# A linear-attention recurrence's decays and bonus sums moved into the stages beside them, and its triangular inverses laid out by the parity of the head

## The chip, the cores and the metric

The kernel runs on one core of a Trainium2 chip. Its time is the device time of one execution in microseconds; a kernel is timed several times and the median stands for it. Lower is better. A profiled execution is one such run with the hardware profiler on.

## The reference, cut to what matters

The program is a block of one layer (a mix of sliding-window attention and an RWKV-7 recurrence, then a gated feed-forward) followed by two more layers. All is float32, 512 tokens, width 1024. The change touches the recurrence of layer one alone:

```python
def rwkv7_time_mix(p, ...):                       # p: 512 tokens x 1792 columns of the projection
    r, k, v, zw, za, zg = jnp.split(p, RWKV_SPLITS, axis=-1)
    w_log = -jax.nn.softplus(-(w0 + jnp.tanh(zw) @ w_decay_up)) - 0.5
    decay = jnp.exp(-jnp.exp(w_log))
    a = jax.nn.sigmoid(a0 + za @ w_iclr_up)
    g = jax.nn.sigmoid(zg) @ w_gate_up
    kk = normalised (k * k_k) per head of 64
    k = k * (1.0 + (a - 1.0) * k_a)
    def step(state, inp):                         # 8 heads, state 64 x 64 each
        sa = einsum('bhvk,bhk->bhv', state, -kk_t)
        state = state * w_t + sa * (kk_t * a_t) + v_t * k_t
        return state, einsum('bhvk,bhk->bhv', state, r_t)
    o = normalised per head, times ln_x_g plus ln_x_b
    bonus = jnp.sum(rh * kh * r_k, axis=-1, keepdims=True) * vh
    return (o + bonus) * g
```

The kernel does the recurrence in 8 chunks of 64 tokens. Inside a chunk the state's own feedback is a unit lower triangular system of 64 x 64 per head, whose inverse it builds by doubling; r, k, kk and aa (= kk times a) are first scaled by running products of the decays, so that inside a chunk plain matrix products remain.

## The kernel before, in words

Heads come in pairs: partition half q (0 or 1) and column block hh (0 to 3) of a [128, 4, 512] tensor hold head 2*hh+q. A token tile t (0 to 3) has 128 tokens, two chunks c of 64.

`first_stage` (line 1658) is the projection. TensorE (PE) goes through 20 tiles m of 128 output columns, each 8 k-steps of three passes (high and low halves of weights and input: lines 325 to 327). Beside each tile, in an order written out by hand through numbers such as RANK, MIX, KSQUARE and KSUM, run the units of the windowed attention (starting, turning, summing), the low-rank products (L1827), the running sums of the log decays (L2034, `scanned`), a's scaling of k (L2036, L2038), and kk's normalisation: squares on ScalarE (ACT, L1959), a head-wise sum on PE with the constant `pair` (L1836, at tiles 16 to 19), a lower bound on VectorE (DVE, L2042), Ln and Exp on ACT (`root`), and two products on DVE (`unit_key`, L1994 and L1995), the last of them after the loop. PE waits for `bounded(i)` before the head-wise sum i, for i of 1 and more. ACT makes the high half of the weights two tiles ahead (L308), GpSimd (POOL) the low half from it (L312), SyncE (SP) loads them.

`rwkv` (line 1263) is three stages with a barrier between each. The first (c1, lines 1269 to 1308) makes the decays' exponentials ep and em on ACT, the last column of each chunk pc, the sigmoid of the gate, on DVE r*r_k*k (L1300), kk times ep and aa times em (L1304, L1305), on PE the head-wise bonus sums (L1295) and on DVE their product with v (L1308).

The second (c2, from line 1314) runs a list `order` of (kind, t, level). Step n uses the PSUM bank pair n mod 4, and PE waits until step n-4 is taken out. A step's 64 x 64 products are issued in the order CROSSED; DVE or ACT (kinds in BY_ACT) take the result out. nt is aa with kk (row half q, column half c of PE, bank q), masked; p0 turns nt by 16 products with the identity, and DVE masks it and adds the identity matrix in a second instruction (L1514, L1515); POOL makes the other orientation Tt from nt in two instructions a tile (L1374, L1376), after its k times em and r times ep (L1370, L1371). Eight `turn` steps bring v, k, aa and kk to token rows (L1418) with ACT copies of 1024 columns. Then come five doubling levels: p (nt with T, masked by DVE, L1517), tt (added by DVE, L1519), t (T is Tt turned by 16 products with the identity, copied by ACT, L1555; not at the last level). p, tt, t, p0, y and u use row half c and column half c only, so halves (0,0) and (1,1) in turn. After them ak (like nt, for k), y, w and u lead into the loop over the 8 chunks (lines 1459 to 1499), in which PE also carries a share of the output projection (`half_tile`, L1448 to L1450). The third stage (from line 1567) normalises and gates.

CROSSED before walks the four halves in two runs, so 8 products go to (0,0) and (1,1) in turn, then 8 to (0,1) and (1,0):

```python
CROSSED = [(x, y, hh) for two in (((0, 0), (1, 1)), ((0, 1), (1, 0))) for hh in range(4) for x, y in two]
```

Of the kernel before, what the change touches and what calls it, by code (L numbers as in the profile page):

```python
# [7 lines left out]
ALU = mybir.AluOpType  # L8
# [121 lines left out]
def _program(nc, a, out, whole):  # L130
# [1132 lines left out]
    def rwkv(r, k, v, zg, aa, kk, decay, oT, attended, f):  # L1263

        with ExitStack() as ctx:
            cs, ep, em, vt = (sb(ctx, n, [P, 4, S]) for n in ("cs", "ep", "em", "vt"))
            masks = sb(ctx, "masks", [P, 10, C])
            pc = sb(ctx, "pc", [P, 4, NCH])
            with ExitStack() as c1:
                s_in, expd, pr, bsum = (sig(n) for n in ("s_in", "expd", "pr", "bsum"))  # L1270
                block = c1.enter_context(stage())

                def ends(m):
                    return ep[:, m, :].rearrange("p (c t) -> p c t", t=C)

                @block.sync
                def _(sp):
                    cst_dma(sp, masks[:, :, :].rearrange("p l n -> p (l n)"), "packed", s_in)
                    sp.wait_ge(s_in.h, 16)

                @block.scalar
                def _(act):
                    for m in range(4):
                        act.activation(ep[:, m, :], decay[:, m, :], ACT.Exp, scale=-EHALF).then_inc(expd.h, 1)
                        act.activation(em[:, m, :], decay[:, m, :], ACT.Exp, scale=EHALF).then_inc(expd.h, 1)
                    for m in range(4):
                        act.wait_ge(expd.h, 2 * m + 1)
                        act.activation(pc[:, m, :], ends(m)[:, :, C - 1], ACT.Copy)
                    act.activation(zg[:, :], zg[:, :], ACT.Sigmoid)

                @block.tensor
                def _(pe):
                    for m in range(4):
                        pe.wait_ge(pr.h, m + 1)
                        pe.matmul(bank[4 + m][:, :], pair, cs[:, m, :], start=True, stop=True).then_inc(bsum.h, 1)  # L1295

                @block.vector
                def _(dve):
                    for m in range(4):
                        pr.by(dve.scalar_tensor_tensor(cs[:, m, :], r[:, m, :], col("r_k", m), k[:, m, :], ALU.mult, ALU.mult))  # L1300
                    for m in range(4):
                        kc = kk[:, m, :].rearrange("p (c t) -> p c t", t=C)
                        dve.wait_ge(expd.h, 2 * m + 2)
                        dve.tensor_tensor(kc[:, :, 1:C], kc[:, :, 1:C], ends(m)[:, :, 0:C - 1], ALU.mult)  # L1304
                        dve.tensor_tensor(aa[:, m, :], aa[:, m, :], em[:, m, :], ALU.mult)  # L1305
                    for m in range(4):
                        dve.wait_ge(bsum.h, m + 1)
                        dve.tensor_tensor(cs[:, m, :], bank[4 + m][:, :], v[:, m, :], ALU.mult)  # L1308
# [6 lines left out]
            with ExitStack() as c2:  # L1315
# [6 lines left out]
                made, took, copied, seeded, uppered, lowered = (  # L1322
                    sig(n) for n in ("made", "took", "copied", "seeded", "uppered", "lowered"))
# [4 lines left out]
                order += [("turn", x, 0) for x in range(8)]  # L1328
# [14 lines left out]
                CROSSED = [(x, y, hh) for two in (((0, 0), (1, 1)), ((0, 1), (1, 0))) for hh in range(4) for x, y in two]  # L1343
# [5 lines left out]
                def at(q, hh):  # L1349
                    return slice(q * HALF + hh * C, q * HALF + hh * C + C)  # L1350

# [17 lines left out]
                def pool_part(pool):  # L1369
                    pool.tensor_tensor(k[:, :, :], k[:, :, :], em[:, :, :], ALU.mult).then_inc(decayed.h, 1)  # L1370
                    pool.tensor_tensor(r[:, :, :], r[:, :, :], ep[:, :, :], ALU.mult).then_inc(decayed.h, 1)  # L1371
                    for t in range(NT):
                        wait_taken(pool, where["nt", t, 0])
                        pool.tensor_tensor(four(Tt[:, t, :]), four(nt[:, t, :]), mask(TURNED), ALU.mult).then_inc(seeded.h, 1)  # L1374
                        pool.wait_ge(seeded.h, 2 * t + 1)
                        pool.tensor_tensor(four(Tt[:, t, :]), four(Tt[:, t, :]), mask(EYE), ALU.add).then_inc(seeded.h, 1)  # L1376
# [8 lines left out]
                def _(sp):  # L1385
                    for c in range(NCH):
# [3 lines left out]
                def _(pe):  # L1390
                    for n, (kind, t, l) in enumerate(order):
# [3 lines left out]
                        if kind == "p0":  # L1395
                            wait_taken(pe, where["nt", t, 0])
# [1094 lines left out]
```

## Time and profile before

| | us |
|---|---|
| median of 3 runs | 2296.46 (2294.19 to 2296.58) |
| the profiled execution | 2295.25 |
| its span, first to last instruction | 2293.5 |
| PE busy in it | 2167.7 (95%) |
| PE weight loads | 1747.6 (76%) |
| DVE busy | 1220.4 (53%) |
| POOL busy | 997.1 (43%) |
| ACT busy | 859.3 (37%) |

Times in the profile are microseconds from the span's start, unless marked ns. A record is one instruction on one engine. A product of fp32 operands leaves two matmul records (PE) and two weight-load records (PEld); a transpose leaves one of each. A record's duration holds its latency, so for products in a stream the distance between starts is what counts.

### The profile page before, as it was taken

To read this page: it belongs to the slowest core of one execution; us is meant where nothing else is said; L and a number is where in the kernel's file an instruction comes from. 1 tells how busy PE (TensorE), PEld (TensorE's weight loads), DVE (VectorE), ACT (ScalarE), POOL (GpSimd) and SP (SyncE) were. 2 spreads that over 40 slices of the span, in tenths; PEclk is the share of its full clock that TensorE was granted. 3 is DMA by queue.
4 is the path that set the end of the run, shared out by engine and by line. 5 is a ranking of instruction groups with operands and counts; after the bars stand their busy time and mean duration, and the time that the engine had idled before them with its cause. 6 is when DMAs were issued, how large, how long until landed. Compare 5 with 4: busy or idle time off the path is not lost. (4 is left out here: it accounts for less than half of the span.)

```text
span 2293.5 us, 35211 instructions
## 1 busy us (share of the span) xinstructions
PE 2167.7 (95%) x13161; PEld 1747.6 (76%) x13161; DVE 1220.4 (53%) x1928; ACT 859.3 (37%) x1345; POOL 997.1 (43%) x524
## 2 busy tenths in 40 slices
PE   6997998799999999899889999999999889999998
PEld 4676985688888888777667888888677668888887
DVE  3456525677505772331774577721397664777601
ACT  3455124433313332332364433332323744333322
POOL 4224011244544444365653444444365734444442
PEclk9998998799999999899999999999999989999999
DMA  4220012133332333333102333333332003333232
GB/s 126 65 65 25 4 32 58 57 101 101 109 92 83 99 93 101 87 83 81 48 1 74 92 91 100 96 94 94 86 86 80 1 20 92 96 101 96 87 101 87
DMA packets 347085, 177.10 MB, mean 77 GB/s; under 512 B 20835, under 2 KB 344158, under 8 KB 346974
## 3 DMA queue, kind: packets, MB, share of 16 engines
q1 hardware_dynamic: 346476, 175.47, 26.7%
q8 instruction: 75, 1.23, 0.2%
q14 instruction: 36, 0.29, 0.0%
q10 hardware_dynamic: 210, 0.08, 0.0%
q0 software_dynamic: 288, 0.03, 0.0%
HBM read 173.44 MB, written 2.11 MB: 77 GB/s over the span
## 5 line engine op out<-in xcount | busy, mean ns | idle before, releaser
L312 POOL TENSOR_TENSOR wlo<-raw,whi 128x1024 fp32r<-128x1024 f32 (+3 forms) x347 | 792.3, 2285 | 1085.4 <-ACT whi L871 605.8
L325 PE MATMUL banks<-xhi,whi 128*128 128x512 f32 x1688 | 669.3, 396 | 6.7 <-DVE cb L1034 3.9
L326 PE MATMUL banks<-xlo,whi 128*128 128x512 f32 x1688 | 659.0, 390 | 0.0
L327 PE MATMUL banks<-xhi,wlo 128*128 128x512 f32 x1688 | 659.0, 390 | 0.0
L325 PEld LDWEIGHTS banks<-xhi,whi 128*128 128x128 f32 x1688 | 318.2, 189 | 82.4 <-issue 13.7
L326 PEld LDWEIGHTS banks<-xlo,whi 128*128 128x128 f32 x1688 | 318.3, 189 | 68.5 <-issue 3.9
L327 PEld LDWEIGHTS banks<-xhi,wlo 128*128 128x128 f32 x1688 | 318.0, 188 | 67.3
L961 ACT ACTIVATE cb<-banks,conv 128x512 f32<-128x512 f32 x152 | 118.0, 779 | 440.8 <-DVE banks L1023 440.8
L871 ACT ACTIVATE whi<-raw 128x1024 fp32r<-128x1024 f32 (+2 forms) x208 | 205.0, 989 | 186.2 <-DMA raw<-in_ffn_w_out_dram 80.6
L325 PE MATMUL banks<-ghi,whi 128*128 128x512 f32 x608 | 236.5, 389 | 0.0
L327 PE MATMUL banks<-ghi,wlo 128*128 128x512 f32 x608 | 236.5, 389 | 0.0
L326 PE MATMUL banks<-glo,whi 128*128 128x512 f32 x608 | 236.5, 389 | 0.0
L1023 DVE TENSOR_TENSOR banks<-banks,rs 128x512 f32<-128x512 f32 x152 | 106.0, 699 | 171.6 <-PE banks L327 154.2
L1042 DVE CAST ghi<-gv 128x512 f32 (+1 forms) x76 | 167.1, 2199 | 10.4 <-DVE gv L1040 2.6
L308 ACT ACTIVATE whi<-raw 128x1024 fp32r<-128x1024 f32 (+3 forms) x139 | 134.6, 970 | 61.8 <-DMA raw<-in_ffn_w_out_dram 22.2
L326 PEld LDWEIGHTS banks<-glo,whi 128*128 128x128 f32 x608 | 114.2, 188 | 23.8
L325 PEld LDWEIGHTS banks<-ghi,whi 128*128 128x128 f32 x608 | 114.1, 188 | 23.6
L327 PEld LDWEIGHTS banks<-ghi,wlo 128*128 128x128 f32 x608 | 114.2, 188 | 23.6
L1034 DVE SCALAR_TENSOR_TENSOR cb<-banks,conv,cb 128x510 f32<-128x510 f32 x152 | 113.8, 749 | 18.3 <-DVE cb L1032 0.3
L1032 DVE SCALAR_TENSOR_TENSOR cb<-banks,conv,cb 128x511 f32<-128x511 f32 x152 | 112.7, 741 | 7.2 <-ACT cb L961 7.2
L1065 DVE TENSOR_TENSOR xT<-banks,xT 128x512 f32 x16 | 11.1, 692 | 191.5 <-PE banks L327 191.5
L1144 POOL TENSOR_SCALAR ex<-ex,mx 128x128 f32<-128x128 f32 (+3 forms) x64 | 70.9, 1122 | 37.9 <-DVE mx L1222 37.9
(450 smaller groups left out, 2619.4 us busy)
## 6 DMA issues: line engine op xcount, KB each, us to landing
raw<-in_ffn_w_in_dram SPq DMA_DIRECT2D x88, 512.0 KB, 3.9
raw<-in_w_ffn_up_dram SPq DMA_DIRECT2D x64, 512.0 KB, 4.1
raw<-in_w_ffn_down_dram SPq DMA_DIRECT2D x32, 512.0 KB, 3.8
raw<-in_ev_w_in_dram SPq DMA_DIRECT2D x25, 512.0 KB, 3.9
raw<-in_ffn_w_out_dram SPq DMA_DIRECT2D x32, 384.0 KB, 3.4
raw<-in_ffn_w_out_dram SPq DMA_DIRECT2D x32, 320.0 KB, 3.3
raw<-in_od_w_in_dram SPq DMA_DIRECT2D x20, 512.0 KB, 3.9
raw<-in_w_in_dram SPq DMA_DIRECT2D x16, 512.0 KB, 3.8
```

The costliest lines, as they stand in the source:

```text
L308: w_hi.by(act.activation(whi[s % CUT][:, 0:n, :], raw[s % RAW][:, 0:n, :], ACT.Copy))
L312: return pool.tensor_tensor(wlo[c][:, 0:n, :], raw[b][:, 0:n, :], whi[c][:, 0:n, :].bitcast(F32), ALU.subtract)
L325: pe.matmul(acc, whi[b][:, k, :], hi(k), start=first and k == 0, stop=False)
L326: pe.matmul(acc, whi[b][:, k, :], lo(k), start=False, stop=False)
L327: mm = pe.matmul(acc, wlo[b][:, k, :], hi(k), start=False, stop=last and k == n - 1)
L871: act.activation(whi[s % CUT][:, 0:n, :], raw[s % RAW][:, 0:n, :], ACT.Copy).then_inc(w_hi.h, 1)
L961: act.activation(cb[j][:, :], bank[j][:, :], ACT.Identity, scale=conv[:, 2, bass.ds(c, 1)], bias=conv[:, 3, bass.ds(c, 1)])\
L1023: dve.tensor_tensor(bank[j % 4][:, :], bank[j % 4][:, :], rs, ALU.mult).then_inc(scaled.h, 1)
L1032: chain(dve.scalar_tensor_tensor(cb[j][:, 1:S], bank[j][:, 0:S - 1], conv[:, 1, bass.ds(c, 1)], cb[j][:, 1:S], ALU.mult, ALU.add))
L1034: dve.scalar_tensor_tensor(cb[j][:, 2:S], bank[j][:, 0:S - 2], conv[:, 0, bass.ds(c, 1)], cb[j][:, 2:S], ALU.mult, ALU.add).then_inc(conve ...
L1042: dve.tensor_copy(ghi[:, i * 2 + q, :], gv[q][:, :]).then_inc(upper.h, 1)
L1144: ins = pool.tensor_scalar(e[:, g, 0:w], e[:, g, 0:w], mx[u % 4][:, 2, g:g + 1], None, ALU.mult)
```

## The change

In `first_stage`: the head-wise sums for kk go from tiles 16 to 19 to tiles 14 to 17 (KSUM 14), so the last `root` and `unit_key` run at tile 18, and the table load for Ln and Exp goes from tile 17 to tile 14. New beside the tiles: r*r_k*k into cs on DVE at tiles 13, 14, 16 and 18; at tiles 15 and 16 ep and em of column blocks 0 and 1 and their part of pc on ACT; one tile later kk times ep and aa times em on DVE; at POOL's turns 18 and 19 k times em and r times ep of a block; the gate's sigmoid as a Tanh on ACT and a scaling on DVE. cs shares its memory with qT.

In `rwkv`: stage c1 is gone. c2 begins with ep and em of blocks 2 and 3 on ACT, kk times ep and aa times em on DVE; PE waits for both blocks (keyed 2), and POOL scales k and r of both blocks. The bonus sums are two steps `bonus` of `order`, evacuated by DVE. p0 is the product of kk and aa in swapped roles instead of a turn of nt. nt, T and pm have the parity of the head as partition half where the products allow it; Tt comes from T, and T from Tt, by four 128 x 128 transposes and one ACT copy of 512 columns; POOL's eight instructions for Tt are gone. nt, p0 and p use all four halves of PE in turn (MIRRORED, PAIRED), and CROSSED, which tt, y, w, u, ak and two places of the chunk loop use (L1475, and L1495 with L1498), is one walk of all four:

```diff
-                order += [("turn", x, 0) for x in range(8)]
+                order += [("turn", 0, 0), ("turn", 1, 0), ("bonus", 0, 0), ("bonus", 1, 0), ("turn", 6, 0), ("turn", 7, 0)]
+                order += [("t", t, 0) for t in range(NT)]
+                order += [("turn", x, 0) for x in (4, 5, 2, 3)]
...
-                CROSSED = [(x, y, hh) for two in (((0, 0), (1, 1)), ((0, 1), (1, 0))) for hh in range(4) for x, y in two]
+                CROSSED = [(x, y, hh) for hh in range(4) for x, y in ((0, 0), (1, 1), (0, 1), (1, 0))]
+                MIRRORED = [(q, hh, c) for c in range(2) for i in range(2) for q, hh in ((0, 2 * i), (1, 2 * i + 1), (0, 2 * i + 1), (1, 2 * i))]
+                PAIRED = [(x % 2, c, x // 2 // 2, 2 * (x // 2 % 2) + x % 2) for i in range(4)
+                          for x, c in ((2 * i, 0), (2 * i + 1, 1), (2 * i, 1), (2 * i + 1, 0))]
...
+                    pool.wait_ge(expd.h, 4)
+                    pool.tensor_tensor(k[:, 2:4, :], k[:, 2:4, :], em[:, 2:4, :], ALU.mult).then_inc(decayed.h, 1)
+                    pool.tensor_tensor(r[:, 2:4, :], r[:, 2:4, :], ep[:, 2:4, :], ALU.mult).then_inc(decayed.h, 1)
...
+                pe.wait_ge(keyed.h, 2)
...
+                        elif kind in ("nt", "p0"):
+                            x, y = (aa, kk) if kind == "nt" else (kk, aa)
+                            for q, hh, c in MIRRORED:
+                                mm = pe.matmul(two[q][part(hh % 2), hh // 2 * P + c * C:hh // 2 * P + (c + 1) * C],
+                                               x[part(q), hh, toks(t, c)], y[part(q), hh, toks(t, c)], start=True, stop=True)
...
+                        elif kind == "t":
+                            for x in range(4):
+                                mm = pe.transpose(two[0][:, x * P:(x + 1) * P], (Tt if l else T)[:, t, x * P:(x + 1) * P], ident)
+                        elif kind == "p":
+                            for x, c, q, hh in PAIRED:
+                                mm = pe.matmul(two[x][part(c), (2 * q + hh // 2) * C:(2 * q + hh // 2 + 1) * C],
+                                               nt[part(x), t, side(q, hh, c)], T[part(x), t, side(q, hh, c)], start=True, stop=True)
...
+                    for i in (2, 3):
+                        dve.wait_ge(expd.h, 2 * i - 2)
+                        later = chunks(kk[:, i, :])[:, :, 1:C]
+                        dve.tensor_tensor(later, later, chunks(ep[:, i, :])[:, :, 0:C - 1], ALU.mult)
+                        dve.tensor_tensor(aa[:, i, :], aa[:, i, :], em[:, i, :], ALU.mult).then_inc(keyed.h, 1)
...
+                        if kind == "bonus":
+                            ins = dve.tensor_tensor(cs[:, 2 * t:2 * t + 2, :], banks[:, 2 * (n % 4):2 * (n % 4) + 2, :], v[:, 2 * t:2 * t + 2, :], ALU.mult)
...
+                            if t == 6:
+                                wait_taken(act, where["bonus", 1, 0])
...
-            RANK, MIX, KSQUARE, KSUM = 6, 8, 13, 16
+            RANK, MIX, KSQUARE, KSUM = 6, 8, 13, 14
+            BONUS, EXPS = (13, 14, 16, 18), 15
...
-                    if m == UNITS + 1:
+                    if m == RANK + 8:
                         act.preload_act_table_set("natural_log_exp_and_others")
```

## Rows read from the trace of the kernel before

**Rows 1.** Windows: stretch, its length, busy us (records) by engine, PE clock, DMA.
```profile
206.90:213.80 6.90, 5.78 (x164) 5.81 (x166) 3.86 (x7) 2.19 (x4) 5.51 (x2) 0.51 0.02 5
213.80:217.00 3.20, 2.87 (x100) 2.73 (x94) 3.05 (x2) 0.00 (x0) 3.20 (x1) 1.00 0.00 0
281.10:296.80 15.70, 13.68 (x519) 12.99 (x515) 3.29 (x6) 7.40 (x13) 0.00 (x0) 1.00 0.02 4
```

**Rows 2.** Timeline, inverses' stage: start, length, engine, line, tiles, count [idle before].
```profile
208.02 4.26 PE L1422 MATMUL banks<-kk,aa 64*64 64x64 f32 x122 [3.34 <-PEq L150]
...
212.80 4.52 POOL L1371 TENSOR_TENSOR r<-r,ep 128x2048 f32<-128x2048 f32 x1
...
214.64 3.23 DVE L1515 TENSOR_TENSOR f<-f,masks 128x512 f32<-128x512 f32 x1
...
225.02 1.93 ACT L1551 ACTIVATE em<-banks 128x1024 f32<-128x1024 f32 x2
225.65 1.91 PE L1418 MATMUL banks<-cst,kk 128*128 128x128 f32 x16
...
227.49 3.95 PE L1432 MATMUL banks<-f,oT 64*64 64x64 f32 x128
...
228.68 0.69 DVE L1517 TENSOR_TENSOR pm<-banks,masks 128x512 f32<-128x512 f32 x1 [5.77 <-PE banks L1432]
...
236.15 0.60 ACT L1555 ACTIVATE f<-banks 128x512 f32<-128x512 f32 x1 [7.36 <-PE banks L1430]
```

**Rows 3.** Timeline of PE, from ak into the chunk loop.
```profile
282.79 1.22 PE L1422 MATMUL banks<-kk,k 64*64 64x64 f32 x56
...
286.07 2.49 PE L1436 MATMUL banks<-vt,pm 64*64 64x64 f32 x78 [0.55 <-issue]
...
296.87 0.59 PE L1462 MATMUL banks<-z,kk 64*64 64x64 f32 x13 [0.95 <-ACT v L1555]
...
303.97 0.93 PE L1475 MATMUL banks<-r,k 64*64 64x64 f32 x29
```

**Rows 4.** Windows of PE alone: stretch, length, busy us (records), PE clock, DMA.
```profile
266.90:270.85 3.95, 3.85 (x126) 1.00 0.01 4
...
289.85:293.25 3.40, 3.08 (x127) 1.00 0.02 5
...
309.12:310.86 1.74, 1.74 (x68) 1.00 0.00 0
```

**Rows 5.** DMA view of 266.90 to 293.25: GB/s in 40 slices, and the only queue.
```profile
GB/s 0 0 25 0 0 0 0 25 0 0 0 0 0 25 0 0 0 0 0 0 25 0 0 0 0 25 0 0 0 0 25 0 0 0 0 0 25 0 0 0
...
q8 instruction: 7, 0.11, 1.8%
```

**Rows 6.** Timeline around tile 15 of the projection.
```profile
157.29 2.68 POOL L312 TENSOR_TENSOR wlo<-raw,whi 128x1024 fp32r<-128x1024 f32 x1 [3.67 <-ACT whi L308]
157.75 2.50 DVE L2036 TENSOR_SCALAR mixin<-aa,pcol 128x512 f32<-128x512 f32 x1
...
160.01 0.70 PE L1845 MATMUL banks<-kd,qT 64*128 64x256 f32 x4
```

**Rows 7.** Timeline, end of the projection and stage c1.
```profile
180.23 1.28 ACT L1961 ACT_TABLE_LOAD   x1
...
191.23 1.02 PE L1836 MATMUL banks<-sq,cst 128*128 128x512 f32 x2
...
192.95 0.75 DVE L2019 SCALAR_TENSOR_TENSOR v<-banks,pcol,v 128x511 f32<-128x511 f32 x1 [0.76 <-ACT v L1914]
...
196.55 0.69 DVE L1995 SCALAR_TENSOR_TENSOR aa<-aa,kk 128x512 f32<-128x512 f32 x1
...
197.77 0.63 ACT L1284 ACTIVATE ep<-oT 128x512 f32<-128x512 f32 x1 [2.15 <-PEq L150]
197.80 2.74 DVE L1300 SCALAR_TENSOR_TENSOR cs<-r,pcol,k 128x512 f32<-128x512 f32 x4 [0.56 <-PEq L150]
198.31 0.61 ACT L1285 ACTIVATE em<-oT 128x512 f32<-128x512 f32 x1
...
198.61 6.07 PE L1295 MATMUL banks<-cs,cst 128*128 128x512 f32 x8 [5.77 <-DVE cs L1300]
```

More of the change, by code:

```diff
@@ L1261, in _, with rwkv @@
                             exped.by(ins)
-    def rwkv(r, k, v, zg, aa, kk, decay, oT, attended, f):
+    def rwkv(r, k, v, zg, aa, kk, decay, cs, pc, oT, attended, f):
         with ExitStack() as ctx:
-            cs, ep, em, vt = (sb(ctx, n, [P, 4, S]) for n in ("cs", "ep", "em", "vt"))
+            ep, em, vt = (sb(ctx, n, [P, 4, S]) for n in ("ep", "em", "vt"))
             masks = sb(ctx, "masks", [P, 10, C])
[L1268 to L1308, printed above, removed]
@@ L1310, in rwkv, with chunks @@
+            def chunks(x):
+                return x.rearrange("p (c t) -> p c t", t=C)
             kt, bt, at_ = ep, em, v
@@ L1401, in _ @@
                             if l == 1:
-                                pe.wait_ge(seeded.h, 2 * t + 2)
+                                wait_taken(pe, where["t", t, 0])
                         elif kind == "t":
-                            wait_taken(pe, where["tt", t, l])
+                            wait_taken(pe, where["tt", t, l] if l else where["p0", t, 0])
                         elif kind == "y":
@@ L1410, in _ @@
                         two = bank[2 * (n % 4)], bank[2 * (n % 4) + 1]
-                        if kind == "turn":
+                        if kind == "bonus":
+                            for j in range(2):
+                                mm = pe.matmul(two[j], pair, cs[:, 2 * t + j, :], start=True, stop=True)
+                        elif kind == "turn":
                             src = (v, k, aa, kk)[t // 2]
@@ L1539, in _ @@
                 def _(act):
+                    for i in (2, 3):
+                        act.activation(ep[:, i, :], decay[:, i, :], ACT.Exp, scale=-EHALF).then_inc(expd.h, 1)
+                        act.activation(em[:, i, :], decay[:, i, :], ACT.Exp, scale=EHALF).then_inc(expd.h, 1)
+                    act.wait_ge(expd.h, 3)
+                    act.activation(pc[:, 2:4, :], ep[:, 2:4, :].rearrange("p i (c t) -> p i c t", t=C)[:, :, :, C - 1], ACT.Copy).then_inc(expd.h, 1)
                     for kk_ in range(4):
@@ L1553, in _ @@
                             ins = act.activation(wt[:, t, :, :, :], both(pr), ACT.Copy)
+                        elif kind == "t":
+                            ins = act.activation((T if l else Tt)[:, t, :], bank[2 * pr][:, :], ACT.Copy)
                         else:
-                            ins = act.activation(four({"t": T, "y": nt, "u": u0}[kind][:, t, :]), both(pr), ACT.Copy)
+                            ins = act.activation(four({"y": nt, "u": u0}[kind][:, t, :]), both(pr), ACT.Copy)
                         ins.then_inc(copied.h, 1)
@@ L1722, in first_stage @@
             AT_K = [ORDER1.index(("p", 4 + i)) for i in range(4)]
-            RANK, MIX, KSQUARE, KSUM = 6, 8, 13, 16
+            RANK, MIX, KSQUARE, KSUM = 6, 8, 13, 14
+            BONUS, EXPS = (13, 14, 16, 18), 15
+            AT_R = [ORDER1.index(("p", i)) for i in range(4)]
             def low_rank(m):
@@ L1940, in _ @@
                         act.activation(zt[0:HD, :], zt[0:HD, :], ACT.Tanh).then_inc(tanhed.h, 1)
+                    if m == AT_Z + 2:
+                        act.wait_ge(moved.h, AT_Z + 2)
+                        act.activation(zg[:, :], zg[:, :], ACT.Tanh, scale=0.5).then_inc(zgated.h, 1)
                     if m - 1 in AT_K:
```

83 lines of the change are left out of this document (52 added, 31 removed).

## The prediction

> **What bounds the kernel now.** The page's first part comes first: PE is busy for 95% of the span, so only PE's time counts. Where the edits lie that average is false. Read in order of time, PE ends its last projection tile at 191.2, does only the bonus products from 198.6 and begins the inverses at 208.0 [rows 2, 7]: 17 us with little in them. From 208.0 its clock is 1.2 GHz until 213.8, then 2.4 GHz [rows 1].
>
> In the doubling levels PE seems full: 128 records in 3.95 us, last latency 0.22 included, so (3.95 - 0.22)/127 = 29.4 ns a record and 0.94 us a step of 32 records (16 products) [rows 2]. Those steps use two halves of PE. The ak step uses all four, in two runs, and goes at (1.22 - 0.22)/55 = 18.2 ns [rows 3], so runs on different halves overlap. L1475, same order, averages 25.4 ns [rows 3].
>
> A second limit stands behind the halves. PE stops at 266.9 and six times after it, marked "issue", as at 286.07 [rows 3]. Between stops lie 126 or 127 matmul records, with their weight loads 256 instructions; the seven pieces end at 293.25, (293.25 - 266.90)/7 = 3.76 us each [rows 4]. In the same stretch the instruction queue brings seven blocks, evenly spaced [rows 5]. I read this as instruction supply: a block of 256 per 3.76 us, whatever PE could do. Even ak, whose 128 records need 2.3 us, is held to it.
>
> **The tail of the projection.** Four head-wise sums of kk move from tiles 16 to 19 to tiles 14 to 17. Each costs PE 0.9 (two records of 0.43) [rows 7]; four now stand ahead of the last tile's end instead of three, +0.9. PE must wait at tile 15 for `bounded`. DVE's tile 14 ends at 160.3 + 0.7 now, because L2036 is blocked behind POOL's weight split [rows 6]. In the change the table load (1.28, rows 7) stands ahead of the weights' high half, so POOL's split moves from 157.3 to some 159.3 and ends at 161.7; it blocks the new bonus product (0.69, a fourth of 2.74 in rows 7) instead, done at 162.3, and `bounded` at 163.0. PE would be ready at 160.0 + 0.9 = 160.9 [rows 6]: a stall of 2.1. Bounds: 0 if the bonus product gets ahead of POOL, 3 if another product of POOL falls in. The other new DVE work (two bonus products, 2 x 2 decays of 0.69) makes DVE one to two us late at tiles 17 and 18, which the distance between tiles hides, (191.2 - 160.0)/4 = 7.8 us [rows 6, 7]; POOL's four new products end before it is next needed. So the last tile ends at 191.2 + 0.9 + 2.1 = 194.2. After it no unit key is left, only scaling, tap and mix: 193.70 - 191.23 = 2.5. The stage ends at 196.7 instead of 197.24.
>
> **The c1 stage goes, and a wait comes.** ACT's first exponential now starts at 196.7 + 0.5 = 197.2. As in c1 the four take 0.54, 0.54, 0.52 and 0.6 [rows 7], so ep and em of block 2 are there after 1.15, of block 3 after 2.2. DVE does kk and aa of block 2 from 1.2 to 2.5. At 2.3 POOL is released by the same em. That DVE instructions with two operands in SBUF stand still for a whole POOL instruction is seen at 214.64: 3.23 us for 0.69 of work, until POOL's product of r ended at 217.3 [rows 2]. POOL's products have half of that size, 2.3. So POOL's k from 2.5 to 4.8, kk of block 3 to 5.4, POOL's r to 7.7, aa of block 3 to 8.35, and all of PE stands behind that wait. PE begins at 197.2 + 8.35 = 205.5 instead of 208.0: **gain 2.5**. Bounds: if DVE keeps its place, PE begins 4.7 earlier.
>
> **From nt to the first level** (now 227.5 - 208.0 = 19.5). nt and p0 run cold, 0.9 a step over four halves, against 4.04/121 x 32 = 1.07 now [rows 2]. The eight are done after some 7 us, but DVE takes p0 with two instructions a tile, 1.45, from 5.0 to 10.8. bonus 1 waits for the last: two fp32 products of 512 columns, 1.7, DVE's take-out 1.3 and 0.5 latency, 14.4. Only then may ACT overwrite v: six turns at 0.93 (two take 1.93, rows 2, less overlap) and four t copies of 0.55 make 7.8, to 22.2. That is when tile 3's p may start, 1.4 after a level's normal start, so level one starts at 20.9: **loss 1.4**. Bounds: loss 3, gain 1. POOL's eight instructions go off-path; their work is now in t.
>
> **Levels and ak to u** (227.5 to 296.9 = 69.4 now). Without the supply limit: p takes 0.47 a step (four halves, twice 29.4 ns' rate), 1.9 for four; tt, which keeps two halves, 3.75; t is four transposes at (1.91 - 0.27)/15 = 0.109, 0.44 a step, 1.75 [rows 2]. DVE takes a step in 0.69 and ACT in 0.60 [rows 2], inside the ring of four. A level is 7.4 instead of 11.2. With the limit: records are 128 + 128 + 16 = 272 a level, four times, 256 for the last, 512 for ak, y, w and u: 1856 = 14.5 blocks, against 2304 = 18.0 now (18 x 3.76 = 67.7, close to the 69.4 seen). One and a half blocks are in store after the slow turns, so 0.9 + 13 x 3.76 + 1.9 = 51.7, with the drain before the chunk loop (0.95 and a copy, rows 3) 1.3, and 1 for waits inside: 54.1. **Gain 15.3**: nearly all of it because t issues fewer instructions, not because p is faster. Bounds: 20.6 (no supply limit: four levels of 7.4, the last 1.9 + 3.75, ak and w at 0.6 a step by DVE's and ACT's pace and y and u at 0.94, 12.3, and the drain: 48.8) and 8.1 (first rival but one).
>
> The Trainium skill (Runtime: NRT & Kernel Launch, Instruction fetch mechanics) says that blocks of 256 instructions are fetched while the current one executes, and that this is hidden. The block's size agrees with the 256 counted between stops; "hidden" does not agree with stops at each of them. By the page the sum would be the upper bound, 20.6.
>
> **Chunk loop.** PE is the bound there. L1475's 32 records take 0.8 at its 25.4 ns [rows 3]; at ak's best rates or a little under them 0.5: 8 x 0.3 = 2.4. L1495 and L1498 take 1.74 for 64 records [rows 4]; now halves change every four products, overlap where they change: 1.2, four times 0.5. **Gain 4.5**, bounds -1.5 and 6.
>
> **Sum.** 2.5 - 1.4 + 15.3 + 4.5 = 20.9. From the profiled execution's 2295.25 (span 2293.5) that is 2274.4; the median is 1.2 above that execution, so **2275.5**. What follows after the third stage is unchanged; the clock's fall there can shift by 1 to 2 us.
>
> **Rivals.**
> - *The lock at the start of c2 doesn't bite.* DVE's four instructions stand back to back, so POOL may have to wait for them. Against: L2036 was blocked by a POOL instruction that came while DVE was at work [rows 6]. Gain 4.7 more: 2271.
> - *Supply is no limit*: the stops come from something else, or blocks are in store. For: no stops before 266.9. Gain 5.3 more: 2270.
> - *The new order overlaps nothing*: overlap comes from whole runs meeting, and alternation by single products is served strictly in order, 0.94 a step. p, nt, p0 gain nothing, ak and L1475 slow to 29.4 ns. Levels 4 x (3.75 + 3.75 + 1.75) + 7.5 = 44.5, ak to u 16.8: gain 8.1 instead of 15.3; chunks -1.5 instead of 4.5. Sum 7.7: 2289. For it: nothing in the trace alternates four halves by single products.
> - *Slower: neighbours in one row half exclude each other.* In the new order the load for (0,1) comes while (0,0) streams. If it must wait, each row half does load and stream in series: a 128-column transpose takes 109 ns [rows 2], so half of that, 55, for a record's stream, and some 27 for its load; over two row halves 41 ns a record, 1.31 a step. Twenty p steps make levels 52.2, ak to u 19.2: 71.4, loss 2; L1475, L1495 and L1498 lose 8 x 0.5 + 4 x 0.9 = 7.6; nt and p0, cold, lose 5. With 2.5 - 1.4: 13.5 slower, 2310. It decides from 33 ns a record on. Against: ak's 18.2 ns includes changes from (0,0) to (0,1) without such a price. The Trainium skill (TensorE: Matmul & The Clock Gate, Part 3) states this rule, that a weight load overlaps a running product only where the row group differs; by it ak would have been slower than p, and the rows say the reverse.
>
> **How the numbers follow.** The forecast holds with 0.51, its own range 2271 to 2281; lock rival 0.15, supply rival 0.12, no-overlap rival 0.13, row rival 0.04; 0.05 for a mix of stalls that ends between 2281 and 2292. Range for 8 in 10, from both fast rivals together to the no-overlap one: 2265 to 2289. A measurement tells 0.2% (4.6 us) from no change: faster 0.94, same 0.02, slower 0.04.
>
> **What would show it.** No stage between projection and inverses; PE's wait at tile 15 (2.1); PE's wait ended by DVE's aa at 8 us after ACT's exponential, with a DVE instruction of over 2 us; ak and p pieces near 15 to 18 ns a record; levels of some 8 us with "issue" stops every 128 matmul records from the first level on, and 54 us from first p to the chunk loop; 0.5 for L1475. Wrong would be p at 29 ns or above, levels of 7.4 without stops, or a time above 2289 or below 2265.

## The result, and the profile after

The changed kernel takes 2275.82 us (median of five runs, 2275.18 to 2276.84); the kernel before, run beside it, 2294.19 (2287.83 to 2296.58). The ratio is 0.9926 with a 95% interval of 0.9914 to 0.9939: 17 us faster, 14 to 20. The forecast of 2275.5 is met, but not every term of it, and part of the agreement is luck, as the table shows. It goes by the starts of the same instructions in both traces: VectorE's scaling of tile 12, ScalarE's first exponential behind the projection, the first product of nt, of level one, of the chunk loop, and of the third stage.

| stretch, us | before | after | difference | forecast |
|---|---|---|---|---|
| up to tile 12 | 136.4 | 139.3 | +2.9 | 0 |
| tile 12 to the exponential | 61.4 | 63.6 | +2.2 | -0.6 |
| exponential to nt | 10.2 | 3.7 | -6.5 | -1.9 |
| nt to level one | 19.5 | 21.3 | +1.8 | +1.4 |
| level one to the chunk loop | 69.4 | 60.5 | -8.9 | -15.3 |
| chunk loop to the third stage | 57.0 | 51.8 | -5.2 | -4.5 |
| third stage to the end | 1939.6 | 1934.9 | -4.7 | 0 |

The five stretches that the change can reach, all but the first and the last row, give 16.6 us instead of 20.9. The first and last row hold unchanged code. Over the fourteen profiled kernels of this case tile 12 is scaled at 135.5 to 139.3 and the last stretch takes 1929.4 to 1939.6, at mean granted clocks over the span of 0.971 to 0.978; so one profiled execution tells nothing of a few us there, and the net 1.8 that these two rows add is not the change's.

The page's busy times after; PE is busy for 2140.0 of 2275.1 us:

```profile
PE 2140.0 (94%) x12729; PEld 1721.0 (76%) x12729; DVE 1224.0 (54%) x1927; ACT 857.7 (38%) x1347; POOL 987.8 (43%) x520
```

Tile 15 in the changed kernel, answering to [rows 6] (timelines of DVE, POOL and PE):

```profile
162.51 2.75 DVE L2063 SCALAR_TENSOR_TENSOR cs<-r,pcol,k 128x512 f32<-128x512 f32 x1
165.18 0.68 DVE L2067 TENSOR_SCALAR roots<-banks 128x512 f32<-128x512 f32 x1
...
162.22 2.49 POOL L312 TENSOR_TENSOR wlo<-raw,whi 128x1024 fp32r<-128x1024 f32 x1 [5.68 <-ACT whi L308]
...
166.01 1.10 PE L1845 MATMUL banks<-sq,cst 128*128 128x512 f32 x2 [2.16 <-DVE roots L2067]
```

This is the stall of the forecast, of the forecast size (2.16 for 2.1): the bonus product lasts 2.75 us, until just after the end of POOL's weight split, for the 0.74 that it takes at 196.83 below; the bound (L2067) stands behind it, PE behind that.

The end of the projection and the start of the inverses' stage, answering to [rows 7]:

```profile
196.83 0.74 DVE L2063 SCALAR_TENSOR_TENSOR cs<-r,pcol,k 128x512 f32<-128x512 f32 x1
198.00 0.69 DVE L2012 SCALAR_TENSOR_TENSOR kk<-kk,mixin 128x512 f32<-128x512 f32 x1 [0.42 <-ACT mixin L1917]
198.73 1.65 DVE L2013 SCALAR_TENSOR_TENSOR aa<-aa,kk 128x512 f32<-128x512 f32 x1
200.41 0.70 DVE L2018 TENSOR_TENSOR banks<-banks,rs 128x512 f32<-128x512 f32 x1
201.86 0.75 DVE L2037 SCALAR_TENSOR_TENSOR v<-banks,pcol,v 128x511 f32<-128x511 f32 x1 [0.75 <-ACT v L1923]
204.09 0.68 DVE L1487 TENSOR_TENSOR kk<-kk,ep 128x504 f32<-128x504 f32 x1 [1.48 <-ACT em L1529]
204.69 0.69 DVE L1488 TENSOR_TENSOR aa<-aa,em 128x512 f32<-128x512 f32 x1
205.29 0.68 DVE L1487 TENSOR_TENSOR kk<-kk,ep 128x504 f32<-128x504 f32 x1
205.88 0.68 DVE L1488 TENSOR_TENSOR aa<-aa,em 128x512 f32<-128x512 f32 x1
...
198.56 1.26 POOL L312 TENSOR_TENSOR wlo<-raw,whi 128x512 fp32r<-128x512 f32 x1 [5.88 <-ACT whi L308]
206.81 2.38 POOL L1346 TENSOR_TENSOR k<-k,em 128x1024 f32<-128x1024 f32 x1 [6.99 <-issue]
...
204.48 0.61 ACT L1529 ACTIVATE em<-oT 128x512 f32<-128x512 f32 x1
...
197.21 0.39 PE L327 MATMUL banks<-xhi,wlo 128*128 128x512 f32 x1
...
206.62 3.69 PE L1396 MATMUL banks<-kk,aa 64*64 64x64 f32 x128 [8.44 <-DVE aa L1488]
```

Two things differ from the forecast. VectorE scales the last tile (L2018) at 200.41, though PE's last product of it, from 197.21 on, is done at 197.6: the last unit key stands before it, its second product (198.73, 1.65 us) once more held by a split. And VectorE's four decay products (204.09 to 206.57) are not blocked: POOL's product of k, released when the last exponential ends at 205.09, begins only at 206.81.

The levels, answering to [rows 2] and [rows 3] (timeline of PE):

```profile
227.90 2.19 PE L1407 MATMUL banks<-f,oT 64*64 64x64 f32 x128
229.91 1.92 PE L1413 MATMUL banks<-f,pm 64*64 64x64 f32 x60
232.35 2.21 PE L1413 MATMUL banks<-f,pm 64*64 64x64 f32 x68 [0.52 <-issue]
234.49 1.97 PE L1404 MATMUL banks<-cst,f 128*128 128x128 f32 x16
236.39 2.10 PE L1407 MATMUL banks<-f,oT 64*64 64x64 f32 x128
...
266.49 0.62 PE L1407 MATMUL banks<-f,oT 64*64 64x64 f32 x26 [1.35 <-issue]
...
270.54 1.03 PE L1413 MATMUL banks<-f,pm 64*64 64x64 f32 x28 [0.57 <-issue]
...
274.27 0.63 PE L1400 MATMUL banks<-kk,k 64*64 64x64 f32 x27 [1.18 <-issue]
...
278.33 1.09 PE L1415 MATMUL banks<-vt,pm 64*64 64x64 f32 x30 [0.63 <-issue]
...
282.34 0.63 PE L1419 MATMUL banks<-f,v 64*64 64x64 f32 x28 [1.46 <-issue]
...
286.16 1.27 PE L1417 MATMUL banks<-oT,f 64*64 64x64 f32 x33 [0.41 <-issue]
...
288.39 0.59 PE L1441 MATMUL banks<-z,kk 64*64 64x64 f32 x13 [0.95 <-ACT v L1553]
```

p (L1407) takes 2.19 for 128 records, (2.19 - 0.22)/127 = 15.5 ns each, about half of [rows 2]; t (L1404) 1.97 with its latency. But level one to level two is 8.49, and from 266.49 to 286.16 the restarts after stops are 3.93 us apart (3.73 to 4.06). One sign of the forecast came only in part: up to 266.49 PE stops once in two blocks (restarts at 232.35, 240.37, 248.66, 257.17 and 266.49, so 4.27 us a block), and at each block only from there on.

### The profile page after: what moved, and what is told of

The parts are those of the page before. It is cut to its first block and busy times, and to the rows that moved or that the text cites. A ratio compares the mean times of both kernels' runs of the same rounds, so it can differ in the third digit from the quotient of the medians.

```text
span 2275.1 us, 34323 instructions
## 1 busy us (share of the span) xinstructions
PE 2140.0 (94%) x12729; PEld 1721.0 (76%) x12729; DVE 1224.0 (54%) x1927; ACT 857.7 (38%) x1347; POOL 987.8 (43%) x520
## 5 line engine op out<-in xcount | busy, mean ns | idle before, releaser
L327 PEld LDWEIGHTS banks<-xhi,wlo 128*128 128x128 f32 x1688 | 318.1, 188 | 67.2
```

The costliest lines, as they stand in the source:

```text
L327: mm = pe.matmul(acc, wlo[b][:, k, :], hi(k), start=False, stop=last and k == n - 1)
```

## The experiments

Each kernel is the changed one with the edit shown; the times in the third column stand beside runs of the kernel before on the same chip.

| kernel | median us | ratio to before | tile 12 to exponential | to nt | to level one | to ak | to chunk loop | to third stage |
|---|---|---|---|---|---|---|---|---|
| changed kernel | 2275.82 | 0.9926 [0.9914, 0.9939] | 63.6 | 3.7 | 21.3 | 43.5 | 17.0 | 51.8 |
| bonus after bound | 2271.36 | 0.9911 [0.9889, 0.9933] | 61.7 | 3.7 | 21.3 | 43.7 | 15.7 | 51.8 |
| key after scaling | 2272.08 | 0.9917 [0.9899, 0.9935] | 62.7 | 3.7 | 21.3 | 41.3 | 15.6 | 51.8 |
| turns, bonus first | 2270.30 | 0.9904 [0.9885, 0.9923] | 63.7 | 8.3 | 14.8 | 41.7 | 16.5 | 51.9 |
| old order of halves | 2280.23 | 0.9947 [0.9930, 0.9964] | 63.6 | 3.7 | 21.3 | 42.2 | 17.0 | 57.0 |
| t twice | 2278.18 | 0.9938 [0.9921, 0.9956] | 63.6 | 3.7 | 20.1 | 46.6 | 16.7 | 51.9 |
| p twice | 2291.82 | 0.9997 [0.9987, 1.0007] | 63.6 | 3.7 | 21.3 | 60.9 | 16.8 | 51.8 |
| gap before block 3 | 2270.82 | 0.9900 [0.9882, 0.9918] | 65.0 | 4.3 | 20.9 | 42.9 | 15.6 | 51.8 |
| inverses and order alone | 2278.67 | 0.9938 [0.9920, 0.9956] | 61.4 | 10.3 | 21.5 | 42.4 | 17.0 | 51.8 |
| block 3 behind POOL | 2273.82 | 0.9920 [0.9902, 0.9939] | 63.6 | 9.6 | 19.7 | 42.1 | 15.7 | 51.8 |
| even spread | 2274.22 | 0.9923 [0.9909, 0.9936] | 63.6 | 3.7 | 13.2 | 51.0 | 16.2 | 51.9 |
| spread, bonus, key | 2267.32 | 0.9895 [0.9880, 0.9910] | 60.6 | 3.7 | 13.2 | 50.9 | 15.7 | 51.8 |
| spread to the stops | 2268.11 | 0.9885 [0.9869, 0.9901] | 60.6 | 3.7 | 12.1 | 51.0 | 17.5 | 51.8 |

How finely this can be read: the changed kernel and four of these (bonus after bound, key after scaling, gap, block 3) have the same PE instructions from nt to the chunk loop, and that stretch took 81.8, 80.6, 78.2, 79.4 and 77.4 us. So where instructions are fetched, one profile is good to 2 us to either side; the projection's columns and the chunk loop's repeat within 0.1, the gap kernel's 65.0 apart. The intervals of the ratios are 5 to 10 us wide. Even they claim too much: the gap kernel, which only adds a wait to the changed one, has the lower ratio (0.9900 [0.9882, 0.9918] for 0.9926 [0.9914, 0.9939]). So what an edit does is read here from the stretches, and a few us between two medians tell nothing.

### Where the order of the halves pays

```diff
-CROSSED = [(x, y, hh) for hh in range(4) for x, y in ((0, 0), (1, 1), (0, 1), (1, 0))]
+CROSSED = [(x, y, hh) for two in (((0, 0), (1, 1)), ((0, 1), (1, 0))) for hh in range(4) for x, y in two]
```

> The changed kernel with the list CROSSED as before (two halves for eight products, then the other two), so that only nt, p0, p keep the new orders. Theory: the chunk loop (chunk loop's first step to the third stage: 57.0 us before, 51.8 in the changed kernel) owes its 5.2 us to this order: 57 again; the step for r's products 0.75 to 0.88 us instead of 0.46 to 0.53. From level one to the chunk loop nothing changes by more than 1 us, since tt uses two halves in either order and ak, y, w, u are held by the supply of instructions. 2281. Rival: the chunk loop is shorter for another reason (its instructions are there in time since fewer were issued before it): then it stays at 52 and the time at 2276.

The chunk loop goes from 51.8 back to 57.0, and level one to ak, 42.2, stays. PE by line in the chunk loop's stretch, of the changed kernel and then of this one (busy, mean ns):

```profile
L1474 PE MATMUL banks<-pm,vt 64*64 64x64 f32 x128 | 4.4, 226 | 0.0
L1477 PE MATMUL banks<-pm,v 64*64 64x64 f32 x128 | 4.2, 218 | 0.0
L1454 PE MATMUL banks<-r,k 64*64 64x64 f32 x128 | 3.2, 222 | 0.0
```

```profile
L1474 PE MATMUL banks<-pm,vt 64*64 64x64 f32 x128 | 7.2, 224 | 0.0
L1477 PE MATMUL banks<-pm,v 64*64 64x64 f32 x128 | 7.0, 218 | 0.0
L1454 PE MATMUL banks<-r,k 64*64 64x64 f32 x128 | 4.4, 221 | 0.0
```

The records are equally long (218 to 226 ns); they overlap more. The order alone is worth 5.2 us, all of it in the chunk loop: shown.

### What bounds the levels

```diff
-for x in range(4):
+for x in 2 * tuple(range(4)) if l else range(4):
```

> The changed kernel with each step t of levels one to four issuing its four transposes twice into the same banks (same result, 8 instructions more a step). The stretch from level one to the chunk loop takes 60.5 us in the changed kernel. Theory (supply of instructions bounds the levels): 4 levels x 4 steps x 8 = 128 instructions, half a block of 256, so 1.9 us more for PE work of 16 x 0.44 = 7.0 us: 62.4, time 2278. Rival (PE's own work bounds them): 7.0 more, 67.5, time 2283. In between if the stops lie where they do for another reason.

```diff
-for x, c, q, hh in PAIRED:
+for x, c, q, hh in 2 * PAIRED:
```

> The changed kernel with each step p of the five levels issuing its 16 products twice into the same banks (same result). PE's own work grows by 20 x 0.46 = 9.2 us, instructions by 20 x 64 = 1280, five blocks of 256. Theory (supply bounds the levels, 3.84 us a block by the fetches in the changed kernel's trace): 60.5 us becomes 60.5 + 19.2 = 79.7, time 2295, with one stop for each 256 instructions. Rival (PE's work bounds them, and the stops are worth only what the trace marks): 60.5 + 9.2 = 69.7, time 2285. Together with the kernel that repeats t: by supply the ratio of the two costs is 10, by PE's work 1.3.

p twice costs 17.2 us from level one to the chunk loop (77.64 for 60.49; 19.0 against 58.6, the mean of the five kernels named above) for 9.2 us of PE work. It adds five blocks of 256 instructions, so 3.4 to 3.8 us a block: the supply's price, not the work's. Here a level's p, now two blocks long, runs into a stop at each block (timeline of PE):

```profile
236.23 2.67 PE L1407 MATMUL banks<-f,oT 64*64 64x64 f32 x167
240.20 1.51 PE L1407 MATMUL banks<-f,oT 64*64 64x64 f32 x89 [1.29 <-issue]
...
244.18 2.89 PE L1413 MATMUL banks<-f,pm 64*64 64x64 f32 x90 [1.32 <-issue]
```

t twice, half a block but 7.0 us of work, costs 63.3 - 60.5 = 2.8 (4.7 against that mean): well under 7.0, and 0.9 to 2.8 more than 1.9, where one profile leaves 2 us open. Supply bounds the stretch, but some of the work seems to come on top, which the forecast's sum (all instructions, divided by 256, at one price) has no room for. The place of long steps was to show why.

```diff
-order += [("turn", 0, 0), ("turn", 1, 0), ("bonus", 0, 0), ("bonus", 1, 0), ("turn", 6, 0), ("turn", 7, 0)]
+order += [("turn", 0, 0), ("turn", 1, 0)]
 order += [("t", t, 0) for t in range(NT)]
-order += [("turn", x, 0) for x in (4, 5, 2, 3)]
+spread = [("bonus", 0, 0), ("bonus", 1, 0)] + [("turn", x, 0) for x in (6, 7, 4, 5, 2, 3)]
 for l in range(1, LEVELS):
     for kind in ("p", "tt", "t") if l < LEVELS - 1 else ("p", "tt"):
         order += [(kind, t, l) for t in range(NT)]
+        if kind != "t" and spread:
+            order += [spread.pop(0)]
```

> The changed kernel with two bonus steps and six of the eight turns taken out of the stretch before level one and put one by one behind the p and tt steps of levels one to four; only the turns of v and t stay ahead. Theory (supply of instruction blocks bounds the levels, PE idles some 13 us in them): nt to level one goes from 21.3 to 12.5 us, VectorE's take-out of p0 being the bound there; level one to the chunk loop grows only by these steps' 96 instructions, 0.4 block or 1.5 us, from 60.5 to 62 (41.3 to 43.7 and 15.6 to 17.0 were seen for its two parts, so 57 to 62 is the same): 7 us sooner, 2269. Rival (PE's own work bounds the levels): their 9.2 us of work are added, 69.7, and nothing is won: 2276.

Nt to level one came out as expected (13.2 for 12.5), but level one to the chunk loop took 67.2: the rival's 69.7 is nearer than the theory's 62. Level two is now PE's own work without a stop (timeline of PE):

```profile
229.18 2.10 PE L1409 MATMUL banks<-f,oT 64*64 64x64 f32 x128
231.21 1.09 PE L1394 MATMUL banks<-cst,kk 128*128 128x128 f32 x8
232.23 3.95 PE L1415 MATMUL banks<-f,pm 64*64 64x64 f32 x128
236.11 1.09 PE L1394 MATMUL banks<-cst,kk 128*128 128x128 f32 x8
237.04 1.94 PE L1406 MATMUL banks<-cst,f 128*128 128x128 f32 x16
238.90 2.15 PE L1409 MATMUL banks<-f,oT 64*64 64x64 f32 x128
```

The DMA view says how the supply works. Changed kernel, 266.4 to 286.4 (40 slices of 0.5 us):

```profile
GB/s 0 0 33 0 0 0 0 0 0 0 33 0 0 0 0 0 0 0 33 0 0 0 0 0 0 33 0 0 0 0 0 0 0 0 33 0 0 0 0 0
...
q8 instruction: 5, 0.08, 2.1%
```

Five blocks, each fetched about 1 us after PE restarts (267.4, 271.4, 275.4, 278.9 and 283.4 after 266.49, 270.54, 274.27, 278.33 and 282.34), and none in between. I read this so: PE's entering a block sets off the fetch of the next, and a block costs the larger of its own work and some 3.9 us. Time that one block has over is not kept for another: a tt block (3.75 of work) fills its time, and a long step beside it is paid in full; only p's blocks (1.9) have room. That reading is from the rows; I did not test it with a long step in the middle of p, and the next kernel has a block that does not fit it.

```diff
+spread = {("tt", 1): ("bonus", 0, 0), ("tt", 2): ("bonus", 1, 0), ("tt", 3): ("turn", 6, 0), ("tt", 4): ("turn", 7, 0)}
...
+for x, kind in zip((2, 3, 4, 5), ("ak", "y", "w", "u")):
+    order += [("turn", x, 0)] + [(kind, t, 0) for t in range(NT)]
```

> As the last version, but the long steps stand where the stops are: in the kernel with the even spread PE had no stop left in levels one to four (9.8 us a level, its own work) and still five of 0.6 to 1.8 us in level five, ak, y, w and u. Here levels one to four hold one bonus step or one turn each (behind tt), and the four turns of k and aa stand one by one ahead of ak, y, w and u. Theory (PE's time in a stretch is the larger of its own work and 3.84 us for each 256 instructions): levels one to four 8.8 us each, level five 7.9, ak to the chunk loop 16 as now, so level one to the chunk loop about 60 instead of 66.6 and nt to the chunk loop 73 to 75 instead of 79.8 (81.8 in the changed kernel); with 3.0 us from the end of the projection 2275.8 - 3.0 - 7 to 8 = 2265. Rival (the total number of instructions up to the chunk loop counts, wherever the long steps stand, since the store fills ahead of level one only as far as it goes): nt to the chunk loop as in the even spread, 79.8, time 2270.

The rival's 79.8 from nt to the chunk loop was right (80.6). The first of the four turns comes ahead of ak's first product; the three behind it cost 17.5 - 15.7 to 16.2 = 1.3 to 1.8 for some 3 of work, so about half of it is hidden. But level one to ak is at 51.0 with five long steps as with eight. Seven stops of 0.3 to 1.9 us are back in it, and one of them shows where the reading above fails (timeline of PE):

```profile
219.29 0.57 PE L1415 MATMUL banks<-f,pm 64*64 64x64 f32 x13 [0.27 <-issue]
...
226.47 0.82 PE L1409 MATMUL banks<-f,oT 64*64 64x64 f32 x36 [1.19 <-issue]
```

The block entered at 219.29 holds a bonus step and t, 6.0 us of work up to 225.3, and by the larger of the two no stop should follow. But in the DMA view the fetch for its successor starts only at 224.0 to 224.5, 4.7 us or more after the entry and not 1, and the stop at its end is 1.19. So the distance from entry to fetch is not fixed; what sets it stays open, and with it why spreading the long steps won nothing.

### The stall at tile 15, and the late scaling

```diff
-if m in BONUS:
-    i = BONUS.index(m)
...
 i = key_of(m, KSUM)
 if i is not None:
     dve.wait_ge(ksummed.h, i + 1)
     bounded.by(dve.tensor_scalar(roots[i % 2][:, :], bank[3][:, :], 1e-24, None, ALU.max))
+if m in BONUS:
+    i = BONUS.index(m)
...
```

> The changed kernel with one edit: in each tile of the projection the bonus product of VectorE stands behind the bound of the squared sum (`bounded`) instead of ahead of it. Theory: at tile 15 it was the bonus product, blocked 2.75 us behind POOL's weight split, that kept `bounded` and so PE waiting; the bound reads PSUM and one operand alone, is not blocked, and PE's wait (163.46 to 166.01, 2.5 us) falls under 0.5. The bonus product is still blocked, but only delays VectorE's next scaling, which has slack. Every later landmark comes 2.1 us sooner, 2273.7. Rival: VectorE's backlog sets the end of the stage anyway (its last key product was blocked once more there), so the wait at tile 15 goes, but the last mix ends as long after tile 12 as now: 2275.8.

The stretch up to the exponential falls by 1.9 (63.6 to 61.7), as the theory had it. VectorE and POOL there:

```profile
159.31 0.69 DVE L2063 TENSOR_SCALAR roots<-banks 128x512 f32<-128x512 f32 x1
159.91 2.14 DVE L2067 SCALAR_TENSOR_TENSOR cs<-r,pcol,k 128x512 f32<-128x512 f32 x1
...
159.01 2.49 POOL L312 TENSOR_TENSOR wlo<-raw,whi 128x1024 fp32r<-128x1024 f32 x1 [5.68 <-ACT whi L308]
```

The bound, under way beside POOL, takes 0.69; the bonus product is still blocked and nobody waits for it. PE's head-wise sum at this tile starts at 160.48, before the last product ahead of it (160.25, 0.40 long) is recorded as done: the wait is gone.

```diff
     scaled.by(dve.tensor_tensor(x[:, :], x[:, :], rs, ALU.mult))
...
+if m == n - 1:
+    unit_key(3)
...
 i = key_of(m, KSUM + 1)
-if i is not None:
+if i is not None and i < 3:
     unit_key(i)
```

> The changed kernel with one edit: VectorE's two products of the last unit key stand behind the scaling of the last tile instead of ahead of it. Theory: in the changed kernel PE's last tile ends at 197.21, but VectorE is held in the last key's product (1.65 us, blocked behind POOL's last split) and scales only at 200.41; that is why the stage ends at 202.6 and not at 199.6 as forecast. With the edit the scaling comes at 197.6, the key products lie under ScalarE's tap, and the mix ends at 200.5: 2.1 us sooner, inverses and all behind them too, 2273.7. Rival: one of the moved products is blocked behind the same split and the mix stands behind it, so that nothing is won: 2275.8.

0.9 instead of 2.1: the scaling comes 2.8 sooner, but the second key product is blocked (1.64) ahead of the mix. With that product behind the mix, in the combined versions, the tail is 60.6, 3.0 less than in the changed kernel with both edits.

### Who blocks whom at the start of the inverses

```diff
 dve.wait_ge(expd.h, 2 * i - 2)
+if i == 3:
+    dve.wait_ge(uppered.h, 1)
```

> The changed kernel with one wait more: VectorE's products of block 3 at the start of the inverses' stage also wait for ScalarE's first copy of the attended part, so that VectorE stands idle for some 0.4 us between block 2 and block 3 after POOL has been released. In the changed kernel VectorE's four products stand back to back and POOL's product of k starts only behind them. Theory (whoever starts first holds the other off; an idle gap lets POOL in): POOL's k starts in the gap, VectorE's next product lasts 2.5 to 3 us instead of 0.68, and the first nt comes 5.5 to 6 us after ScalarE's first exponential, or 8 if POOL's r gets in as well, instead of 3.7; time 2278 to 2280. Rival (VectorE goes ahead of POOL whenever it has work): 0.4 us later only, 4.1 after the exponential, 2276.

> The changed kernel with VectorE's products of block 3 waiting for ScalarE's fourth copy of the attended part. In the kernels run so far POOL's product of k begins 1.72 us after ScalarE's last exponential, whatever VectorE does (also where a gap of 0.4 us stood open to it), so it simply comes after VectorE's four products. Here VectorE's kk of block 3 is released at 4.5 us after the first exponential, when POOL's k (from 3.9 on, 2.4 long) is under way. Theory (a VectorE product with two operands in SBUF stands still for the POOL instruction that started before it, as forecast for this place): kk lasts 2.4 instead of 0.68, and nt begins at 7.6 after the first exponential, or 9.4 if POOL's r gets in before aa. Rival (no such block here): kk and aa 0.7 each, nt at 5.9.

(The second has `uppered.h, 4` in the same place.) In the first, nt comes 4.3 after the exponential: the rival's number, but not for its reason. POOL's k did not come in the gap either: it began 3.9 us after the first exponential, as in the changed kernel (206.81 - 202.91), and now while a VectorE product ran. The second kernel shows the lock with its price:

```profile
203.89 2.30 DVE L1489 TENSOR_TENSOR kk<-kk,ep 128x504 f32<-128x504 f32 x1 [2.02 <-ACT ahi L1535]
206.11 2.82 DVE L1490 TENSOR_TENSOR aa<-aa,em 128x512 f32<-128x512 f32 x1
...
203.31 2.34 POOL L1346 TENSOR_TENSOR k<-k,em 128x1024 f32<-128x1024 f32 x1 [6.99 <-issue]
205.61 2.78 POOL L1347 TENSOR_TENSOR r<-r,ep 128x1024 f32<-128x1024 f32 x1
```

Each product lasts until just after the end of the POOL instruction that was under way when it began, and nt comes at 9.6 (9.4 expected). So the forecast's mechanism exists at this place; POOL was merely 1.7 us late for it. What POOL waits for in that time ("issue") the profile does not show.

### The parts, and an earlier start

> Part of the change alone: the kernel before, with its projection and its stage for exponentials and bonus products as they were, but the new inverses (parity layout, t by transposes, nt and p0 over four quadrants) and the new order of halves. Expected from the ledger of the two traces, as differences to before: levels and ak to u 69.4 to 60.5 (-8.9), chunk loop 57.0 to 51.8 (-5.2), nt to level one 19.5 minus 0.1 (two bonus steps and their take-out, which the changed kernel holds there, are not there: 21.3 - 5 = 16.5, so -3). Sum -17: 2277, so the move of exponentials and bonus products is worth only about 1 to 2 us by itself. Rival: the stage that was dissolved is worth its 8 us (198.3 to 206.3) even net of what it put elsewhere: then this kernel is at 2283 or above.

```diff
+with ExitStack() as c1:
+    s_in, expd, pr, bsum = (sig(n) for n in ("s_in", "expd", "pr", "bsum"))
...
-order += [("turn", 0, 0), ("turn", 1, 0), ("bonus", 0, 0), ("bonus", 1, 0), ("turn", 6, 0), ("turn", 7, 0)]
+order += [("turn", 0, 0), ("turn", 1, 0), ("turn", 6, 0), ("turn", 7, 0)]
...
-pool.tensor_tensor(r[:, 2:4, :], r[:, 2:4, :], ep[:, 2:4, :], ALU.mult).then_inc(decayed.h, 1)
+pool.tensor_tensor(r[:, :, :], r[:, :, :], ep[:, :, :], ALU.mult).then_inc(decayed.h, 1)
```

2278.67: the inverses and the order are most of the change. From tile 12 to the third stage it takes 204.3 us, the kernel before 217.5, the changed one 200.9: the move of bonus products and decays adds 3.4, give or take the 2 us of one profile, where 1 to 2 were expected. One expectation failed: nt to level one is 21.5, not 16.5, though no bonus step is in it. VectorE shows why:

```profile
212.34 4.99 DVE L1531 TENSOR_TENSOR f<-f,masks 128x512 f32<-128x512 f32 x1
...
212.27 4.51 POOL L1384 TENSOR_TENSOR r<-r,ep 128x2048 f32<-128x2048 f32 x1
```

POOL's undivided product of r blocks the take-out of p0; in the changed kernel its halves are mostly past by then.

```diff
-order = [(kind, t, 0) for kind in ("nt", "p0") for t in range(NT)]
-order += [("turn", 0, 0), ("turn", 1, 0), ("bonus", 0, 0), ("bonus", 1, 0), ("turn", 6, 0), ("turn", 7, 0)]
+order = [("turn", 0, 0), ("turn", 1, 0), ("bonus", 0, 0), ("bonus", 1, 0)]
+order += [(kind, t, 0) for kind in ("nt", "p0") for t in range(NT)]
+order += [("turn", 6, 0), ("turn", 7, 0)]
```

> The changed kernel with the two turns of v and the two bonus steps ahead of nt instead of behind p0 (the wait for the decayed keys moves to nt, ScalarE's four copies of the attended part stand behind the first two turns' copies). Theory: PE idles 4 us before nt (202.6 to 206.6), and v and the bonus products are ready then; these four steps take 5 to 6.5 us in the changed kernel (213.36 to 219.83), 4 of which fit in the gap. VectorE then sets the pace from nt on: bonus 2 x 1.3, nt 4 x 0.69, p0 4 x 1.45 = 11.2 from 206.6 give 217.8, then two to four turns: level one starts at 223, 5 us sooner; 2271. Rival A (instruction supply): the levels are held by the supply of instruction blocks, which goes on at its own pace, so an earlier start only lengthens the stops: level one 5 sooner, the ak step under 1 sooner: 2275. Rival B: POOL gets between VectorE's products of decays and bonus, two times 2.4 us, and nt starts 2 to 3 later: 2274.

Exponential to level one goes from 25.0 to 23.1, 1.9 sooner and not 5: the granted clock is 0.58 there (199.2 to 206.4 us of its trace, so mostly 1.2 GHz), the turns of v and the bonus steps take 3.65 and 4.86 us, and they overfill the gap: nt comes 4.5 later.

The version that combines the even spread, the bonus product behind the bound, and the last key around the mix:

```diff
+if m == n - 1:
+    dve.wait_ge(rooted.h, 4)
+    chain(dve.scalar_tensor_tensor(unit_k[:, 3, :], unit_k[:, 3, :], -1.0, roots[1][:, :], ALU.mult, ALU.mult))
 if mixed(m):
...
+if m == n - 1:
+    chain(dve.scalar_tensor_tensor(aa[:, 3, :], aa[:, 3, :], -1.0, unit_k[:, 3, :], ALU.mult, ALU.mult))
```

> The version that the runs point to: the turns and bonus steps spread over the levels, the bonus product behind the bound of the squared sum (1.9 us measured), and VectorE's last unit key behind the scaling of the last tile, its second product behind the mix (1.0 us measured with both ahead of the mix; 0.6 more since aa was the one that POOL's split blocked). Sum with the 7 us of the spread: 2275.8 - 7 - 1.9 - 1.6 = 2265. Rival: as for the spread alone, 2272.

This version and the one with the other spread have the lowest ratios: 0.9895 [0.9880, 0.9910] and 0.9885 [0.9869, 0.9901]. Both intervals lie below the changed kernel's (0.9914 to 0.9939), but not below the gap kernel's. The 3.0 us of the tail are shown; the spread itself, nt to the chunk loop in 79.8 and 80.6 us, lies within the 77.4 to 81.8 of the kernels without it.

## Why the prediction was right, and where it was not

- **Tail of the projection.** The wait at tile 15 was right in place, cause and size; taking the cause away gave back 1.9. What failed is "makes DVE one to two us late at tiles 17 and 18, which the distance between tiles hides": the lateness carried into the last tile, where the last unit key and one more block stand before the scaling. Forecast -0.6, measured +2.2.
- **Exponential to nt.** The forecast 8.3 us was 3.7. The rival with the lock had the number; neither had the reason, POOL's late start. Together with the tail the gain was 4.3 where 2.5 was forecast.
- **Nt to level one.** 1.8 lost, 1.4 forecast: VectorE's take-out of p0 and the bonus steps ahead of ScalarE's last copies, as described.
- **Levels and ak to u.** The mechanism (supply by blocks of 256 instructions, p's speed hidden) was right, the term mis-sized: 8.9 in the profile of the changed kernel (up to 12.5 in those with the same PE instructions) for 15.3. The step that failed is "0.9 + 13 x 3.76 + 1.9", with 3.76 us for every block alike. The one and a half blocks in store were there: the first stop came after 128 + 60 matmul records. But the 13 blocks from the restart at 232.35 to the one at 286.16 took 4.14 each, which is 4.9 of the 6.4 that are missing; the two ends, up to 232.35 and from 286.16 on, took 6.7 for 5.1 (0.9, 1.9, the drain and the waits). In the levels a block costs 4.27, behind them 3.93: by the reading above, since work that does not fit its own block comes on top. That nearly all of the gain comes from t's fewer instructions was argued and not tested: no run changes the form of t alone. The Trainium skill (Runtime: NRT & Kernel Launch, Instruction fetch mechanics) calls this fetch hidden; p twice, 3.4 to 3.8 us a block for 1.9 of work, says that it is not in code this dense.
- **Chunk loop.** 5.2 for 4.5, and all of it the order's. Products on (0,0) and (0,1), one row half, which the slower rival lets exclude each other (41 ns a record), overlap: p takes 15.5 ns a record. The Trainium skill (TensorE: Matmul & The Clock Gate, Part 3) has a weight load overlap only where the row group differs; the order (0,0), (1,1), (0,1), (1,0) changes the row half each time, so these runs don't test that rule itself. Nor do ak's two runs of halves, (0,0) with (1,1) and (0,1) with (1,0), so the forecast's "by it ak would have been slower than p" does not follow.
- **The total.** 16.6 of 20.9 came from the forecast's stretches. That the time came out at 2275.8 all the same is luck: unchanged code differed by 1.8 more between the profiles, and the median of before in these runs was 2.3 lower than the one that the sum started from (2296.46).

## What to carry to other kernels

Where PE runs many small products, count instructions by block: in these traces most blocks of 256 cost the larger of their own work and the fetch's round (3.7 to 4.1 us), so a faster order pays only in blocks whose work is longer than that. An instruction of VectorE with two operands in SBUF should not stand before the one that PE waits for, if POOL's turn comes at that time. And when a stage is dissolved, look at what the last tile's queue holds, since nothing behind it hides lateness.

## What was not expected of the hardware

- POOL answered the release by the last exponential 1.72 us late in all kernels with that wait; in the kernel whose POOL product stands first behind the stage's start it began 0.2 us after VectorE's first instruction there. It does not answer every release so late: in the changed kernel its split at tile 15 began at 162.22, 0.08 us after the end of ScalarE's high half.
- An instruction block was fetched only about 1 us after PE had entered the block before it (once 4.7 or more, in the last of the kernels with spread steps), and restarts were 3.9 us apart although the fetches took little of the DMA (2.1% of the engines' time).
- Four halves of PE, alternated product by product, went at 15.5 ns a record, against 18.2 in two runs of halves [rows 3] and 29.4 on two halves [rows 2].
